# Two alternating single-column Newton chains for the norm's 1/std in a two-layer decoder trunk

## The chip, the cores and the metric

The kernel runs on one core of one Trainium2 chip. The metric is the device time of one execution in microseconds. Lower is better.

## What is computed

The reference is a trunk of two layers over 256 tokens of 2048 features, in float32. Each layer computes three branches from one input product (stick-breaking attention, a diagonal state-space model with a GLU, and cross-attention to 256 memory tokens), merges them with sigmoid gates, multiplies by `w_o`, normalises, then runs a SwiGLU feed-forward part of width 5632 and normalises again. So there are four layer norms, and the change lies in them alone:

```python
def _layer_norm(x, g, b):
    xf = x.astype(jnp.float32)
    mu = jnp.mean(xf, axis=-1, keepdims=True)
    var = jnp.mean(jnp.square(xf - mu), axis=-1, keepdims=True)
    return ((xf - mu) * lax.rsqrt(var + LN_EPS) * g + b).astype(x.dtype)
...
x = _layer_norm(DN_ALPHA * x + mix_out, ln1_g[l], ln1_b[l])
...
x = _layer_norm(DN_ALPHA * x + ffn_out, ln2_g[l], ln2_b[l])
```

## The kernel before

The 256 tokens are two blocks of 128 partitions (`TT = 2`). Weights come in as chunks of 1 MB (`raw`) and are split into a rounded part (`hi`, on ScalarE, L631) and a remainder (`lo`, on VectorE, L986), so that TensorE can multiply float32 values as pairs of faster products; the activations are split in the same way (`xs`). A layer goes through the phases U, BR, BL, GLU, G, WO and FF; FF takes 11 turns. Every engine has its own program, written out by hand, and they meet at semaphores: `.then_inc(s, 1)` raises one when an instruction has completed, `wait_ge(s, n)` holds the engine that waits. Nothing is scheduled by a tool.

The state-space part of BR and BL (`scan_states`, L1208 and on; L1230 and L1238) is of use for reading this change. It runs two independent scans `e = 0, 1` on VectorE, alternating, and each instruction waits only for the instruction of its own scan, two or more positions back. All of its instructions take a `[128, 1]` multiplier from the tile `pw` as a per-partition scalar (called a pointer scalar here); an immediate is a number that stands in the instruction.

A norm stands at the end of WO (`norm(l, 0)`) and at the end of FF (`norm(l, 1)`). On VectorE (`norm`, L1031 and on) it runs as follows. The sums of the last token blocks are added to `rows` and their statistics taken (L1145 or L1143, and L1154). Two `bn_aggr` (L1045) give mean and variance of the two token blocks, `mv[:, m, :]`. From there to the end of the Newton steps all work is on tiles of 128 x 2, one column for each token block: `var` = variance + eps (L1047), a first guess `r` by integer arithmetic on its bits (L1049), and three Newton steps of three instructions (L1051 to L1053), r <- r (1.5 - 0.5 var r r). `lnk` makes each of them raise the semaphore `ln_step` and makes the next one wait for it, so this is one chain:

```python
for _ in range(3):
    lnk(dve.scalar_tensor_tensor(out=t, in0=r, scalar=-0.5, in1=r, op0=ALU.mult, op1=ALU.mult))
    lnk(dve.tensor_tensor(u, t, var, ALU.mult))
    lnk(dve.scalar_tensor_tensor(out=r, in0=u, scalar=1.5, in1=r, op0=ALU.add, op1=ALU.mult))
```

L1071 then makes `rv[:, 4, :]` = -mean r. VectorE normalises token block 0 in six pieces (`centre`, L1079) and ScalarE block 1 (L711, which waits for `LN_STEPS * (v + 1)` counts of `ln_step`). TensorE transposes the normalised rows (`turn`, L1582), VectorE and ScalarE apply gain and bias (L1086, L718) and split (L726, L1091), and the next phase's first products (L1503 to L1505, or L1611 and L1612) follow block by block.

What TensorE does while the norm's statistics are taken differs. In `norm(l, 0)` it has 24 products with an identity whose results nobody reads (L1860). In `norm(0, 1)` it multiplies the memory tokens for the next layer (L1488, L1491). In the last norm, `norm(1, 1)`, there are no transposes: VectorE subtracts the mean and multiplies by the gain (L1058) for six of eight pieces, ScalarE makes a diagonal matrix from r (L955, after `LN_STEPS * 4 - 1` counts), TensorE first puts the bias into its banks (L1880) and then adds the product of that diagonal and the pieces (L1884), ScalarE copies out (L958), SyncE stores (L491). VectorE finishes the other two pieces alone (L1058, L1068, stored at L494).

Of the kernel before, what the change touches and what calls it, by code (L numbers as in the profile page):

```python
# [12 lines left out]
ALU = mybir.AluOpType  # L13
# [4 lines left out]
TT = T // P  # L18
# [51 lines left out]
def chunk_no(ph, l, i, c):  # L70
    return i * len(PHASES[ph][1]) + (l * CH_LAYER + CH_BASE[ph] + c)
# [29 lines left out]
HALF_CREDIT = HLS  # L101
TILE_CREDIT = 2

LN_STEPS = 14
SUMS_WO, SUMS_FF = 6, 4
SUMS_LAYER = SUMS_WO + 11 * SUMS_FF + 2
GATES = ((0, 0, 0), (1, 2, 4), (2, 3, 5))
# [6 lines left out]
def trunk(nc, x, mem, w_in, b_in, sb_w_out, lam_re_d, lam_im_d, log_dt_d, b_re_d, b_im_d, c_re_d,  # L114
# [3 lines left out]
    with ctx:  # L118
# [3 lines left out]
        def sem(name):  # L122
            return ctx.enter_context(nc.semaphore(name))
# [144 lines left out]
        stats_done, ln_step, norm_done, ln_T = sem("stats_done"), sem("ln_step"), sem("norm_done"), sem("ln_T")  # L268
# [12 lines left out]
        def norm_cols(l, which, k):  # L281

            if which == 0:
                return par[:, l, 80 + k:81 + k], par[:, l, 96 + k:97 + k]
            return par[:, 2, 32 * l + k:32 * l + k + 1], par[:, 2, 32 * l + 16 + k:32 * l + 17 + k]
# [4 lines left out]
        def next_chunk(ph, l, i, c):  # L290

            if c + 1 < len(PHASES[ph][1]):
                return ph, l, i, c + 1
            if PHASES[ph][0] > 1:
                return ph, l, i + 1, 0
            return ORDER[ORDER.index(ph) + 1], l, 0, 0
# [49 lines left out]
        def piece(t, m, c):  # L346
            return t[:, m, 512 * c:512 * c + 512]
# [275 lines left out]
        def _(act):  # L623
# [78 lines left out]
            def norm(l, which):  # L702
# [4 lines left out]
                def centre(q):  # L707
                    y = rows[:, 1, CENTRES[q]:CENTRES[q + 1]]
                    if q == 0:
                        act.wait_ge(ln_step, LN_STEPS * (v + 1))  # L710
                    act.activation(y, y, ACT.Identity, bias=rv[:, 4, 1:2], scale=rv[:, 1, 1:2]).then_inc(norm_act, 1)  # L711
# [240 lines left out]

            act.wait_ge(ln_step, LN_STEPS * 2 * DEPTH - 1)
            for m in range(TT):
# [7 lines left out]
        def _(dve):  # L962
# [21 lines left out]
            def lo_half(slot, s, h, gh):  # L984
                dve.wait_ge(hi_ready, gh + 1)
                dve.tensor_tensor(lo[:, s, :], raw[:, slot, h * HALF:(h + 1) * HALF], hi[:, s, :].bitcast(F32),  # L986
                                  ALU.subtract).then_inc(lo_ready, 1)
# [45 lines left out]
            def norm(l, which):  # L1033
                v = 2 * l + which
                base = LN_STEPS * v
                k = [0]

                def lnk(ins):
                    k[0] += 1
                    ins.then_inc(ln_step, 1)  # L1040
                    dve.wait_ge(ln_step, base + k[0])

                dve.wait_ge(stats_done, 8 * v + 8)
                for m in range(TT):
                    lnk(dve.bn_aggr(mv[:, m, :], st[:, m, :, :].rearrange("p a b -> p (a b)")))  # L1045
                var, r, t, u = rv[:, 0, :], rv[:, 1, :], rv[:, 2, :], rv[:, 3, :]
                lnk(dve.tensor_scalar(var, mv[:, :, 1], EPS, None, ALU.add))  # L1047

                lnk(dve.tensor_scalar(r.bitcast(I32), var.bitcast(I32), -0.5, float(0x5f3759df), ALU.mult, ALU.add))  # L1049
                for _ in range(3):  # L1050
                    lnk(dve.scalar_tensor_tensor(out=t, in0=r, scalar=-0.5, in1=r, op0=ALU.mult, op1=ALU.mult))  # L1051
                    lnk(dve.tensor_tensor(u, t, var, ALU.mult))
                    lnk(dve.scalar_tensor_tensor(out=r, in0=u, scalar=1.5, in1=r, op0=ALU.add, op1=ALU.mult))  # L1053
                if v == 2 * DEPTH - 1:

                    def scaled(m, c):
                        y = piece(rows, m, c)
                        dve.scalar_tensor_tensor(out=y, in0=y, scalar=mv[:, m, 0:1], in1=piece(raw, 0, c),  # L1058
                                                 op0=ALU.subtract, op1=ALU.mult).then_inc(dve_affine, 1)

                    dve.wait_ge(gb_in, 32)
                    for j, (m, c, _) in enumerate(PE_PIECES):
                        scaled(m, c)
                    for j, (m, c) in enumerate(DVE_PIECES):
                        scaled(m, c)
                        dve.wait_ge(dve_affine, len(PE_PIECES) + 2 * j + 1)
                        y = piece(rows, m, c)
                        dve.scalar_tensor_tensor(out=y, in0=y, scalar=rv[:, 1, m:m + 1], in1=piece(raw, 1, c),  # L1068
                                                 op0=ALU.mult, op1=ALU.add).then_inc(dve_affine, 1)
                    return  # L1070
                lnk(dve.scalar_tensor_tensor(out=rv[:, 4, :], in0=mv[:, :, 0], scalar=-1.0, in1=r, op0=ALU.mult,  # L1071
                                             op1=ALU.mult))
                assert k[0] == LN_STEPS
                ph, i, c = ("U", 0, 0) if which else ("FF", 0, 0)
                nxt = next_chunk(ph, l + which, i, c)

                def centre(q):
                    y = rows[:, 0, CENTRES[q]:CENTRES[q + 1]]
                    dve.tensor_scalar(y, y, mv[:, 0, 0:1], rv[:, 1, 0:1], ALU.subtract, ALU.mult).then_inc(norm_done, 1)  # L1079

                def affine(k):
                    g, b = norm_cols(l, which, k)
                    dve.wait_ge(ln_T, 16 * v + k + 1)
                    if k >= 4:
                        dve.wait_ge(xs_lo, 16 * v + k - 3)
                    dve.tensor_scalar(xf[:, k % 4, :], bank[k % 4][:, 0:T], g, b, ALU.mult, ALU.add  # L1086
                                      ).then_inc(aff_dve, 1)

                def lo_part(k):
                    dve.wait_ge(xs_hi, 16 * v + k + 1)  # L1090
                    dve.tensor_tensor(xs[:, k, T:2 * T], xf[:, k % 4, :], xs[:, k, 0:T].bitcast(F32), ALU.subtract  # L1091
                                      ).then_inc(xs_lo, 1)

                def split(h):
                    lo_half(PHASES[nxt[0]][1][nxt[3]], hl_slot(ph, c + 1, h), h,
                            chunk_no(ph, l + which, i, c) * 2 + (2 + h))

                def second_pair(h):
                    lo_half(PHASES["FF"][1][2], hl_slot("FF", 2, h), h, chunk_no("FF", l, 0, 2) * 2 + h)

                centre(0)
                centre(1)
                affine(0)
                if which:
                    split(0)
                centre(2)
                for k in range(2, KD, 2):
                    affine(k)
                    lo_part(k - 2)
                    lo_part(k - 1)  # L1110
                    if k < 6:
                        centre(2 + k // 2)
                    if k == 4 and not which:
                        split(0)
                    if k == 8:
                        split(1)
                    if k == 12 and not which:
                        second_pair(0)
                lo_part(KD - 2)
                lo_part(KD - 1)  # L1120
                if not which:
                    second_pair(1)
# [44 lines left out]
            for l in range(DEPTH):  # L1167
# [190 lines left out]
                for t in range(4):  # L1358
# [5 lines left out]
                    if l + t > 0:  # L1364
                        dve.wait_ge(glu_lo, 4 * l + t)
                    dve.scalar_tensor_tensor(out=acc[:], in0=bran[:, 1, :], scalar=1.0, in1=bran[:, 0, :],
                                             op0=ALU.add, op1=ALU.mult).then_inc(glu_m, 1)
                    dve.wait_ge(glu_hi, 4 * l + t + 1)
                    dve.scalar_tensor_tensor(out=ssmT[:, t, T:2 * T], in0=acc[:], scalar=0.5,
                                             in1=ssmT[:, t, 0:T].bitcast(F32), op0=ALU.mult,  # L1370
                                             op1=ALU.subtract).then_inc(glu_lo, 1)
# [26 lines left out]
                for i in range(2):  # L1398
# [9 lines left out]
                    else:  # L1408
                        last_sums("WO", l, 1, 7, 4, 1.0 if l else ALPHA)
                norm(l, 0)  # L1410

                last_l = l == DEPTH - 1
# [60 lines left out]
                with dve.Fori(1, 10) as i:  # L1473
                    ffn_turn(i, False, False)
                ffn_turn(10, False, True)
                norm(l, 1)


# [408 lines left out]
def hl_slot(ph, c, h):  # L1887

    return (2 * c + h) % HLS
# [26 lines left out]
```

## Time and profile before

| | us |
|---|---|
| median of 3 runs | 3010.62 (3010.21 to 3011.47) |
| the profiled execution | 3008.55 |
| its span | 3006.8 |
| TensorE busy | 2958.4 (98%) |
| VectorE busy | 2062.7 (69%) |
| ScalarE busy | 1468.9 (49%) |

The span runs from the first to the last instruction of the profiled execution; the device time of that execution has 1.75 us more around it. Granted clock is the share of the full TensorE clock that the chip allowed, 0.997 over the span. In timelines the first column is the start in us from the span's start, the second the time from the first start to the last end of a merged row, and xN says how many instructions are merged in it.

### The profile page before, as it was taken

How to read it: one execution, taken by the hardware profiler on the slowest of the kernel's cores; microseconds unless marked ns; L12 is line 12 of the kernel's file. 1: busy time of each engine (PE TensorE's matmuls, PEld its weight loads, DVE VectorE, ACT ScalarE, POOL GpSimd, SP SyncE). 2: the span in 40 equal slices, each digit the busy share in tenths (PEclk: the TensorE clock that was granted, in tenths of full speed). 3: DMA queues.
4: the chain of work that ended last, by engine and by line, in shares of the span. 5: the costliest groups of instructions: out<-in, count | busy, mean ns of one | idle time of the engine just before them, and what ended most of it. 6: DMA issues, size and time to landing. Idle time of an engine off the chain costs nothing.

```text
span 3006.8 us, 46802 instructions
## 1 busy us (share of the span) xinstructions
PE 2958.4 (98%) x16222; PEld 2536.1 (84%) x16222; DVE 2062.7 (69%) x3163; ACT 1468.9 (49%) x1975; POOL 129.8 (4%) x191
## 2 busy tenths in 40 slices
PE   6999999999999999999999999999999999999999
PEld 5888888888888888888878888888888888888887
DVE  5999766665766565655699996666767656555666
ACT  4556555454544444444455655555435444444443
POOL 5000011110000000000000000001000000000000
PEclk9999999999999999999999999999999999999999
DMA  8656567676565555555556566776765555555554
GB/s 275 170 157 172 154 181 198 178 206 211 204 204 195 195 188 188 182 195 195 168 155 160 158 169 169 195 194 179 218 218 182 189 188 182 195 195 183 191 186 153
DMA packets 672970, 562.17 MB, mean 187 GB/s; under 512 B 20761, under 2 KB 637569, under 8 KB 671873
## 3 DMA queue, kind: packets, MB, share of 16 engines
q1 hardware_dynamic: 668688, 548.48, 60.5%
q10 hardware_dynamic: 4208, 12.74, 1.1%
q8 instruction: 43, 0.70, 0.1%
q14 instruction: 31, 0.25, 0.0%
HBM read 552.78 MB, written 8.39 MB: 187 GB/s over the span
## 4 chain that ended last, share of the span: by engine, by line
PE 92%; DVE 5%; POOL 1%; ACT 1%; issue 1%; ACTq 0%; DMA 0%; DVEq 0%; POOLq 0%
PE banks L1488 22%; PE banks L1503 22%; PE banks L1491 11%; PE banks L1505 11%; PE banks L1513 7%; PE banks L1514 7%; PE banks L1515 7%; PE banks L1781 2%; DVE lo L986 1%; PE banks L1783 1%; DVE st L1154 1%; DVE scan_t L1230 0%; DVE rows L1143 0%; DVE blocks L1238 0%; POOL sc L317 0%
## 5 line engine op out<-in xcount | busy, mean ns | idle before, releaser
L986 DVE TENSOR_TENSOR lo<-raw,hi 128x1024 fp32r<-128x1024 f32 x1016 | 1222.3, 1239 | 427.5 <-ACT hi L631 397.9
L631 ACT ACTIVATE hi<-raw 128x1024 fp32r<-128x1024 f32 x884 | 904.9, 1053 | 542.1 <-PE banks L1505 288.0
L1503 PE MATMUL banks<-xs,hi 128*128 128x512 f32 x2816 | 886.4, 396 | 2.9 <-DVE xs L1091 2.9
L1488 PE MATMUL banks<-xs,hi 128*128 128x512 f32 x2544 | 807.6, 399 | 6.6 <-DVE lo L986 4.7
L1505 PEld LDWEIGHTS banks<-xs,lo 128*128 128x128 f32 x2816 | 529.0, 188 | 124.8
L1491 PEld LDWEIGHTS banks<-xs,lo 128*128 128x128 f32 x2544 | 479.0, 188 | 113.3
L1505 PE MATMUL banks<-xs,lo 128*128 128x256 f32 x2816 | 553.4, 278 | 0.0
L1491 PE MATMUL banks<-xs,lo 128*128 128x256 f32 x2544 | 501.2, 278 | 0.0
L1503 PEld LDWEIGHTS banks<-xs,hi 128*128 128x128 f32 x2816 | 430.0, 189 | 5.7 <-DVE xs L1091 3.9
L1488 PEld LDWEIGHTS banks<-xs,hi 128*128 128x128 f32 x2544 | 388.9, 189 | 14.6 <-issue 8.2
L1513 PE MATMUL banks<-hi,hT 128*128 128x512 f32 x704 | 274.0, 389 | 0.0
L1514 PE MATMUL banks<-lo,hT 128*128 128x512 f32 x704 | 274.0, 389 | 0.0
L1515 PE MATMUL banks<-hi,hT 128*128 128x512 f32 x704 | 273.9, 389 | 0.0
L656 ACT ACTIVATE tmp<-banks,par 128x256 f32<-128x256 f32 x144 | 68.2, 473 | 328.7 <-PE banks L1491 328.7
L1143 DVE TENSOR_TENSOR rows<-rows,banks 128x1024 f32<-128x1024 f32 (+1 forms) x98 | 109.5, 1152 | 117.7 <-PE banks L1515 117.7
L643 ACT ACTIVATE hi<-raw 128x1024 fp32r<-128x1024 f32 x132 | 134.8, 1052 | 79.6 <-PE banks L1515 79.6
L1515 PEld LDWEIGHTS banks<-hi,hT 128*128 128x128 f32 x704 | 132.2, 188 | 27.5
L1513 PEld LDWEIGHTS banks<-hi,hT 128*128 128x128 f32 x704 | 132.1, 188 | 26.7
L1514 PEld LDWEIGHTS banks<-lo,hT 128*128 128x128 f32 x704 | 132.2, 188 | 26.6
L999 DVE SCALAR_TENSOR_TENSOR gate<-banks,tmp 128x256 f32<-128x256 f32 x96 | 40.8, 425 | 126.6 <-ACT tmp L656 126.6
L937 ACT ACTIVATE pt<-banks 128x512 f32<-128x512 f32 x88 | 52.6, 598 | 152.3 <-PE banks L1505 152.3
L1513 PE MATMUL banks<-hi,mT 128*128 128x512 f32 x256 | 99.9, 390 | 1.5 <-DVE lo L986 1.5
(216 smaller groups left out, 2603.1 us busy)
## 6 DMA issues: line engine op xcount, KB each, us to landing
raw<-in_ffn_w_gate_up SPq DMA_DIRECT2D x176, 1024.0 KB, 5.1
raw<-in_w_in SPq DMA_DIRECT2D x160, 1024.0 KB, 7.6
raw<-in_ffn_w_down SPq DMA_DIRECT2D x88, 1024.0 KB, 5.3
raw<-in_w_o SPq DMA_DIRECT2D x32, 1024.0 KB, 5.3
raw<-in_mem_w_kv SPq DMA_DIRECT2D x16, 1024.0 KB, 5.7
raw<-in_sb_w_out SPq DMA_DIRECT2D x32, 512.0 KB, 4.1
raw<-in_ssm_w_out SPq DMA_DIRECT2D x32, 256.0 KB, 4.5
raw<-in_mem_w_out SPq DMA_DIRECT2D x32, 256.0 KB, 4.8
```

Of the source, the lines that this page charges most:

```text
L631: act.activation(hi[:, hl_slot(ph, c, h), :], raw[:, slot, h * HALF:(h + 1) * HALF], ACT.Copy).then_inc(hi_ready, 1)
L643: act.activation(hi[:, hl_slot(ph, c + 1, h), :], raw[:, slot, h * HALF:(h + 1) * HALF], ACT.Copy).then_inc(hi_ready, 1)
L656: ins = act.activation(tmp[:, k % 2, :], src[:, 0:T], ACT.Identity, bias=bias, scale=scale)
L986: dve.tensor_tensor(lo[:, s, :], raw[:, slot, h * HALF:(h + 1) * HALF], hi[:, s, :].bitcast(F32), ALU.subtract).then_inc(lo_ready, 1)
L1143: dve.tensor_tensor(y2, y2, src, ALU.add).then_inc(rows_out, 1)
L1488: pe.matmul(dst[:, :], hi[:, s, k * P:(k + 1) * P], x_t[:, k0 + k, :], start=first and k == 0, stop=False)
L1491: ins = pe.matmul(dst[:, 0:T], lo[:, s, k * P:(k + 1) * P], x_t[:, k0 + k, 0:T], start=False, stop=last and k == 7)
L1503: pe.matmul(bank[base + j], hi[:, s, at[j]], xs[:, k, :], start=k == 0, stop=False)
L1505: ins = pe.matmul(bank[base + j][:, 0:T], lo[:, s, at[j]], xs[:, k, 0:T], start=False, stop=last)
L1513: pe.matmul(dst, xh, hi[:, s, w], start=first, stop=False)
L1514: pe.matmul(dst, xh, lo[:, s, w], start=False, stop=False)
L1515: return pe.matmul(dst, xl, hi[:, s, w], start=False, stop=last)
```

## The change

The product with the variance moves out of the steps: `u` = -0.5 var is made once (L1050), and a step is then t = r u r (L1056) and r = (t + 1.5) r (L1062). Both are issued for each of the two columns by itself, and `u[:, c]` is now a pointer scalar of L1056. Each instruction waits for all but the one right in front of it, so that the columns form two chains that alternate. The first of all, and what follows behind the last, waits for everything. A norm counts 18 steps instead of 14 (12 + 1 in place of 9), which moves the thresholds that ScalarE waits for.

```diff
-LN_STEPS = 14
+LN_STEPS = 18
...
-                for _ in range(3):
-                    lnk(dve.scalar_tensor_tensor(out=t, in0=r, scalar=-0.5, in1=r, op0=ALU.mult, op1=ALU.mult))
-                    lnk(dve.tensor_tensor(u, t, var, ALU.mult))
-                    lnk(dve.scalar_tensor_tensor(out=r, in0=u, scalar=1.5, in1=r, op0=ALU.add, op1=ALU.mult))
+                lnk(dve.tensor_scalar(u, var, -0.5, None, ALU.mult))
+                for step in range(3):
+                    for m in range(TT):
+                        c = slice(m, m + 1)
+                        dve.wait_ge(ln_step, base + (k[0] if step == 0 and m == 0 else k[0] - 1))
+                        k[0] += 1
+                        dve.scalar_tensor_tensor(out=t[:, c], in0=r[:, c], scalar=u[:, c], in1=r[:, c], op0=ALU.mult,
+                                                 op1=ALU.mult).then_inc(ln_step, 1)
+                    for m in range(TT):
+                        c = slice(m, m + 1)
+                        dve.wait_ge(ln_step, base + k[0] - 1)
+                        k[0] += 1
+                        dve.scalar_tensor_tensor(out=r[:, c], in0=t[:, c], scalar=1.5, in1=r[:, c], op0=ALU.add,
+                                                 op1=ALU.mult).then_inc(ln_step, 1)
+                dve.wait_ge(ln_step, base + k[0])
```

On VectorE, the instructions of the first norm from the first guess to the first normalised piece stand in this order before (`rv` holds var, r, t and u, each of two columns; the names in brackets are the semaphores waited for):

```order
L1049 TENSOR_SCALAR rv<-rv 128x2 [waits ln_step]
L1051 SCALAR_TENSOR_TENSOR rv<-rv 128x2 [waits ln_step]
L1052 TENSOR_TENSOR rv<-rv 128x2 [waits ln_step]
L1053 SCALAR_TENSOR_TENSOR rv<-rv 128x2 [waits ln_step]
L1051 SCALAR_TENSOR_TENSOR rv<-rv 128x2 [waits ln_step]
L1052 TENSOR_TENSOR rv<-rv 128x2 [waits ln_step]
L1053 SCALAR_TENSOR_TENSOR rv<-rv 128x2 [waits ln_step]
L1051 SCALAR_TENSOR_TENSOR rv<-rv 128x2 [waits ln_step]
L1052 TENSOR_TENSOR rv<-rv 128x2 [waits ln_step]
L1053 SCALAR_TENSOR_TENSOR rv<-rv 128x2 [waits ln_step]
L1071 SCALAR_TENSOR_TENSOR rv<-mv,rv 128x2 [waits ln_step]
L1079 TENSOR_SCALAR rows<-rows,mv,rv 128x128 [waits ln_step]
```

The same place in the changed kernel, where later lines have moved down by 11 (L1071 is L1082, L1079 is L1090):

```order
L1049 TENSOR_SCALAR rv<-rv 128x2 [waits ln_step]
L1050 TENSOR_SCALAR rv<-rv 128x2 [waits ln_step]
L1056 SCALAR_TENSOR_TENSOR rv<-rv 128x1 [waits ln_step] x2
L1062 SCALAR_TENSOR_TENSOR rv<-rv 128x1 [waits ln_step] x2
L1056 SCALAR_TENSOR_TENSOR rv<-rv 128x1 [waits ln_step] x2
L1062 SCALAR_TENSOR_TENSOR rv<-rv 128x1 [waits ln_step] x2
L1056 SCALAR_TENSOR_TENSOR rv<-rv 128x1 [waits ln_step] x2
L1062 SCALAR_TENSOR_TENSOR rv<-rv 128x1 [waits ln_step] x2
L1082 SCALAR_TENSOR_TENSOR rv<-mv,rv 128x2 [waits ln_step]
L1090 TENSOR_SCALAR rows<-rows,mv,rv 128x128 [waits ln_step]
```

Nine chained instructions have become thirteen, one of two columns and twelve of one; nothing else on VectorE or on another engine has moved.

## Rows read from the trace of the kernel before

**Rows 1.** The page's busy times and its chain that ended last.
```profile
PE 2958.4 (98%) x16222; PEld 2536.1 (84%) x16222; DVE 2062.7 (69%) x3163; ACT 1468.9 (49%) x1975; POOL 129.8 (4%) x191
...
PE 92%; DVE 5%; POOL 1%; ACT 1%; issue 1%; ACTq 0%; DMA 0%; DVEq 0%; POOLq 0%
```

**Rows 2.** Timeline of the first norm: start us, us, engine, line, operation [idle before <- releaser].
```profile
772.44 5.76 PE L1860 MATMUL banks<-xs,ident_r 128*128 128x512 f32 x24
...
775.63 0.17 DVE L1049 TENSOR_SCALAR rv<-rv 128x2 int32<-128x2 int32 x1
775.83 0.16 DVE L1051 SCALAR_TENSOR_TENSOR rv<-rv 128x2 f32<-128x2 f32 x1
...
777.59 0.16 DVE L1071 SCALAR_TENSOR_TENSOR rv<-mv,rv 128x2 f32<-128x2 f32 x1
777.79 1.80 ACT L711 ACTIVATE rows<-rows,rv 128x128 f32<-128x128 f32 x3 [2.71 <-DVE rv L1071]
...
778.43 0.41 PE L1582 MATMUL banks<-ident,rows 128*128 128x128 f32 x2 [0.23 <-ACT rows L711]
```

**Rows 3.** VectorE groups by line and form: count | busy us, mean ns | idle before.
```profile
L1454 DVE SCALAR_TENSOR_TENSOR hh<-hh,uu 128x512 f32<-128x512 f32 x44 | 30.4, 692 | 4.7
...
L1058 DVE SCALAR_TENSOR_TENSOR rows<-rows,mv,raw 128x512 f32<-128x512 f32 x8 | 5.5, 747 | 0.0
...
L1053 DVE SCALAR_TENSOR_TENSOR rv<-rv 128x2 f32<-128x2 f32 x12 | 1.9, 161 | 0.4
...
L1238 DVE SCALAR_TENSOR_TENSOR blocks<-blocks,pw,scan_t 128x64 f32<-128x64 f32 x320 | 69.3, 278 | 0.0
```

**Rows 4.** VectorE's timeline in one scan, two steps of the two alternating chains.
```profile
202.97 0.62 DVE L1230 SCALAR_TENSOR_TENSOR scan_t<-blocks,pw 128x128 f32<-128x128 f32 x2
203.50 0.88 DVE L1238 SCALAR_TENSOR_TENSOR blocks<-blocks,pw,scan_t 128x64 f32<-128x64 f32 x4
204.28 0.62 DVE L1230 SCALAR_TENSOR_TENSOR scan_t<-blocks,pw 128x128 f32<-128x128 f32 x2
```

**Rows 5.** VectorE's timeline elsewhere: neighbours not chained, without a pointer scalar.
```profile
200.37 0.42 DVE L999 SCALAR_TENSOR_TENSOR qm_f<-banks,tmp 128x256 f32<-128x256 f32 x1
200.70 2.36 DVE L986 TENSOR_TENSOR lo<-raw,hi 128x1024 fp32r<-128x1024 f32 x2
```

**Rows 6.** Timeline of the third norm, TensorE's cover and what follows it.
```profile
2249.43 5.76 PE L1860 MATMUL banks<-xs,ident_r 128*128 128x512 f32 x24
...
2255.41 0.41 PE L1582 MATMUL banks<-ident,rows 128*128 128x128 f32 x2 [0.23 <-ACT rows L711]
```

**Rows 7.** Timeline of the second norm, TensorE's cover and what follows it.
```profile
1519.81 0.39 PE L1491 MATMUL banks<-mT,lo 128*128 128x256 f32 x2
...
1520.84 0.41 PE L1582 MATMUL banks<-ident,rows 128*128 128x128 f32 x2 [0.63 <-ACT rows L711]
```

**Rows 8.** Timeline of the last norm and the end of the kernel.
```profile
2991.44 5.31 PE L1880 MATMUL banks<-raw,ident 128*128 128x512 f32 x12
...
2995.86 4.73 DVE L1058 SCALAR_TENSOR_TENSOR rows<-rows,mv,raw 128x512 f32<-128x512 f32 x7
...
2996.16 0.59 PE L1880 MATMUL banks<-raw,ident 128*128 128x512 f32 x1
2996.76 0.67 PE L1884 MATMUL banks<-rows,diag 128*128 128x512 f32 x1
...
3002.80 0.33 SPq L491 DMA_DIRECT2D out_x<-rows  x1
3003.18 0.96 SPq L494 DMA_DIRECT2D out_x<-rows  x2
```

**Rows 9.** Windows, first and second norm: busy PE, PEld, DVE, ACT, POOL, granted clock, DMA.
```profile
780.00:784.00 4.00, 3.28 (x21) 2.97 (x22) 3.60 (x9) 3.97 (x10) 0.00 (x0) 1.00 0.91 393
...
1520.00:1524.00 4.00, 1.90 (x12) 1.04 (x11) 3.61 (x8) 3.52 (x8) 0.00 (x0) 0.97 0.00 0
1524.00:1528.00 4.00, 3.74 (x17) 3.41 (x18) 3.77 (x10) 3.59 (x8) 0.00 (x0) 0.60 0.00 0
```

## The prediction

> **What bounds the kernel now.** I read the page's busy times and its chain first, then the timelines of the four norms, then the VectorE groups by form, and last a stretch where this kernel already runs two alternating chains. TensorE is busy 98% of the span and holds 92% of the chain that ended last; VectorE holds 5% [rows 1]. The norms belong to those 5%: TensorE cannot go on before they have given it rows. In the first norm the Newton steps run from 775.83 to 777.59 us with no other work on VectorE, ScalarE waits 2.71 us for the instruction behind them, and TensorE starts its transposes at 778.43, released by ScalarE's first piece [rows 2]. So this code is on the path in every norm, and what is won or lost there is won or lost in the time, as long as TensorE's own cover does not end later.
>
> How much there is to win is plain from the same rows: nine instructions in 777.59 - 775.83 = 1.76 us, or 0.196 us each [rows 2]. One takes 0.161 us [rows 3]; 0.035 us more pass until the next one, which waited for it, starts. Four norms hold 4 x 1.76 = 7.0 us, 0.23% of the time. Even if all of it went, the kernel would gain hardly more than the 0.2% (6.0 us) from which a measurement of this kernel can tell a difference from no change.
>
> **The change, part by part.** Removed: nine chained instructions a norm, 1.76 us.
>
> Added, L1050: one two-column instruction with an immediate, chained to both neighbours. Its twin L1049 starts 775.83 - 775.63 = 0.20 us ahead of its successor [rows 2]. **+0.20 us.**
>
> Added, twelve single columns in two chains. This needs two prices for each kind: the latency (how soon an instruction that waits for it can start), and the spacing (how soon any next one can).
>
> *Latency.* L1062 has only immediates and one column. The two-column L1053 takes 0.161 us, and a column costs about (692 - 161) / 510 = 1.04 ns [rows 3], so one column fewer is worth 1 ns: 0.160 + 0.035 = 0.195, say 0.196 us. L1056 has a pointer scalar. With 512 columns that form takes 747 ns against 692 with an immediate, and with 64 columns 278 against 161 + 62 x 1.04 = 226 [rows 3]: 52 to 55 ns more. The trace has no pointer form of one column; I carry 52 ns down to it, 0.160 + 0.052 = 0.212 us, and 0.248 with the wait. Bounds: 0.196 (no surcharge at this width) and 0.248.
>
> *Spacing.* Here the scan is the same code pattern. Two L1230 of 128 columns and four L1238 of 64 make a step, and it takes 204.28 - 202.97 = 1.31 us [rows 4]. The first L1238 starts 0.53 us behind the first of two L1230, so 0.265 us each; the four L1238 take 0.78, or 0.195 each, though one lasts 0.278 [rows 3, 4]. So neighbours overlap by 0.083 us, also those that carry a wait for the other's predecessor. At 1.04 ns a column both spacings are 0.13 us plus the columns; the 512-column L1058 gives (4.73 - 0.75) / 6 = 0.663, also 0.13 plus the columns [rows 8]. Without a pointer scalar the constant is smaller: L986 starts 0.33 us behind L999, which has 256 columns [rows 5]: 0.06 to 0.07. For one column: **0.131 us behind L1056, 0.065 behind L1062.** Whether so small an instruction can follow as closely is unknown; the lower bound is 0.065 for both, the upper one no overlap at all, which is the slow rival below.
>
> *The schedule of a step* (starts in us, t and r for L1056 and L1062, columns 0 and 1). t0 at 0, t1 at 0.131. r0 must be 0.131 behind t1 and 0.248 behind t0: 0.262. r1 must be 0.065 behind r0 and 0.248 behind t1: 0.379. The next t0 waits for r0: 0.262 + 0.196 = 0.458. A step takes 0.458 us against 3 x 0.196 = 0.588 before. The last r1 starts at 2 x 0.458 + 0.379 = 1.295, and L1082 waits for it: 1.295 + 0.196 = 1.49. With L1050 the block takes **1.69 us against 1.76: 0.07 us less a norm.** The saved third instruction is paid back by the pointer scalar, by the offset of the second chain and by L1050.
>
> *What that does behind the block.* In the first norm TensorE's filler products, 24 in all, end at 772.44 + 5.76 = 778.20, and the transposes start at 778.43; the third norm has the same distance, 2255.41 - 2255.19 = 0.22 [rows 2, 6]. So 0.07 passes in full, and nothing above 0.23 would. In the second norm the cover ends at 1520.20 and the transposes start at 1520.84 [rows 7]: room for 0.64. In the last one L1884 starts at 2996.76, 0.15 behind the end of the first L1058 (2995.86 + 0.75), and the last of twelve L1880 starts at 2996.16, (2996.16 - 2991.44) / 11 = 0.43 apart, so it is out of the way by 2996.59: room for 0.17 [rows 8]. The stores follow in SyncE's order, the last two at 3003.18, behind one of 0.33 us issued at 3002.80 that waits for ScalarE, hence for TensorE [rows 8]; VectorE's and TensorE's paths move together. The prefetches, loads and semaphores are unchanged: no queue is passed. ScalarE's new thresholds name the same instructions.
>
> **Sum:** 4 x (1.76 - 1.69) = 0.28 us less. Against the profiled execution that is 3008.55 - 0.28 = 3008.27; that execution was 2.07 us below the median of the runs, so for the median 3010.62 - 0.28 = **3010.3 us**.
>
> **A rule that speaks against it.** The scan's step of 1.31 us holds six pointer instructions whose durations add up to 2 x 0.355 (0.62 less the spacing) + 4 x 0.278 = 1.82 us [rows 3, 4], so they overlap at 64 and 128 columns. The Trainium skill (VectorE: DVE Perf Modes, section on the DRAIN, and its rules for authors) says that a chain of VectorE instructions pays a pipeline flush each whether or not they wait for each other, and to keep the count of operations low rather than that of semaphores; a neighbouring section of the same page lets a following instruction that is not held start earlier. By the first rule thirteen in place of nine can only lose; by these rows it fails at 64 columns, and none shows it at one.
>
> **The rivals.**
> *No overlap at one column (slower).* Every one of the twelve waits out its predecessor as if chained: 6 x 0.248 + 6 x 0.196 + 0.20 = 2.86 us, 1.10 more than before; four norms give +4.4 us, 3015.0. For it: every short instruction in this trace that stands close to others is chained, so none shows an overlap; the skill's rule would give this. Against: [rows 4]. Two periods stand in the block, so it breaks even when a step takes 0.458 + 0.07 / 2 = 0.49 us; four durations end to end (2 x 0.212 + 2 x 0.160 = 0.74) would be far beyond that. A loss has no cover in any norm and passes in full.
> *Cheap columns (faster than I say).* No pointer surcharge and 0.065 spacing: period 0.392, last r1 at 0.784 + 0.261, the block 1.44 us, 0.32 less. TensorE's covers cut this to 0.23 + 0.32 + 0.23 + 0.17 = 0.95 us: 3009.7. Against: the surcharge is the same at 64 and 512 columns, so it is not one per column.
> *The clock.* In the second norm the granted clock falls to 0.60 in 1524 to 1528 [rows 9], behind a stretch of 4 us in which TensorE was busy 1.90. That is a stretch mostly at 1.2 instead of 2.4 GHz; 4 us at a mean of 0.60 do the work of 2.4, so a dip costs at most 1.6 us. A start that moves by 0.07 us could end this dip or bring one in another norm: 3008.7 or 3011.9. Against: in the first norm the same place ran at 1.00 [rows 9], and 0.07 us is little beside the idle time there, 4.00 - 3.28.
> *Nothing moves at all* is not apart from the forecast in the time; the trace would tell them apart.
>
> **How the numbers follow.** Overlap as in the scan, 0.28 us less: 0.72. Cheap columns: 0.08. No overlap, +4.4: 0.10. The clock, 1.6 either way: 0.08. Something unseen: 0.02. The range starts from the runs themselves, since 0.28 us is smaller than their own spread: the lowest time seen for this kernel is 3008.55 and the highest 3011.47. Low: 3008.55 - 0.28, rounded to 3008.3. High: 3011.47 + 1.6 = 3013.1. It leaves out the case without overlap, and no more than a tenth beside it. All cases lie within 6.0 us of before, so the chances are 0.01 faster, 0.97 same, 0.02 slower, the last for a cost that no row shows.
>
> **What would show it.** In the changed profile: L1056 at about 212 ns and L1062 at 160, the start of the first L1056 to the start of L1082 1.49 us, a step 0.46; L1082 to the first transpose unchanged at 0.84 us; in each norm the transposes 0.07 earlier behind the last statistics. Starts of neighbours 0.25 and 0.20 apart throughout would show the first rival; 0.07 apart the second. Wrong altogether would be a block longer than 1.76 us, or a time outside the range with a block near 1.69, which would put the cause elsewhere.

## The result and the profile after

| | before | changed |
|---|---|---|
| median of 6 runs, us | 3011.05 (3009.03 to 3012.36) | 3022.64 (3020.33 to 3025.82) |
| ratio, 95% interval | | 1.0039 (1.0029 to 1.0049) |
| span of the profiled execution, us | 3006.8 | 3024.1 |

By the medians the change makes the kernel 11.6 us slower (0.39%). The forecast was 3010.3 us, 0.28 us faster, with a range of 3008.3 to 3013.1. The two profiled executions lie 17.3 us apart, because that of before was among the fastest of its kernel and that of the changed kernel the slowest of its own (3025.82).

The place that was forecast first. VectorE's timeline of the first norm in the changed kernel, which answers to [rows 2]:

```profile
778.88 0.17 DVE L1049 TENSOR_SCALAR rv<-rv 128x2 int32<-128x2 int32 x1
779.09 0.17 DVE L1050 TENSOR_SCALAR rv<-rv 128x2 f32<-128x2 f32 x1
779.37 0.35 DVE L1056 SCALAR_TENSOR_TENSOR rv<-rv 128x1 f32<-128x1 f32 x2
779.63 0.28 DVE L1062 SCALAR_TENSOR_TENSOR rv<-rv 128x1 f32<-128x1 f32 x2
779.84 0.34 DVE L1056 SCALAR_TENSOR_TENSOR rv<-rv 128x1 f32<-128x1 f32 x2
...
780.55 0.28 DVE L1062 SCALAR_TENSOR_TENSOR rv<-rv 128x1 f32<-128x1 f32 x2
780.86 0.16 DVE L1082 SCALAR_TENSOR_TENSOR rv<-mv,rv 128x2 f32<-128x2 f32 x1
```

From the first L1056 to L1082 it is 780.86 - 779.37 = 1.49 us, as forecast, and two chains do run side by side: two L1056 of 0.215 us each (the groups below) end within 0.35. But 0.28 us pass from L1050 to L1056, not 0.20. The block takes 1.77 us where before took 1.76: the change gains nothing at its own place and loses nothing there. The 11.6 us are elsewhere.

The trace's records have one instruction more here than the order listing ahead of the prediction, which isn't counted as busy and so stands in no timeline: a wait by itself (L1054) between L1050 and the first L1056. `lnk` puts a wait behind L1050, and the first turn of the step loop puts the same wait ahead of L1056; an instruction carries one of the two, the other becomes an instruction of its own. So a norm has not four instructions more but five.

I looked for the 11.6 us with the waits. VectorE's waits in which the profile shows nothing that it waited for, first before, then changed (line waited: us in total, times, longest):

```profile
DVE sp_t L1246 <- issue: 5.3, 8, 0.8
DVE scan_t L1230 <- issue: 1.4, 2, 0.7
DVE pw L1257 <- issue: 0.8, 4, 0.2
```
```profile
DVE pw L1268 <- issue: 14.5, 4, 7.3
DVE sp_t L1257 <- issue: 5.0, 7, 0.8
DVE scan_t L1241 <- issue: 1.4, 2, 0.7
```

L1257, now L1268, is the first copy in the body of the branch loop (`dve.Fori(0, 3)`, phase BR). The change doesn't touch it. Its two long waits are at the two branches back of layer 1. VectorE's timeline before:

```profile
1603.98 0.42 DVE L999 SCALAR_TENSOR_TENSOR u_f<-banks,tmp 128x256 f32<-128x256 f32 x1
1604.39 0.42 DVE L1251 TENSOR_TENSOR sbT<-banks,sbT 128x256 f32 x1
...
1605.02 0.21 DVE L1257 COPY pw<-powers 128x96 f32 x1 [0.20 <-issue]
...
1669.72 0.42 DVE L999 SCALAR_TENSOR_TENSOR u_f<-banks,tmp 128x256 f32<-128x256 f32 x1
...
1735.47 0.42 DVE L999 SCALAR_TENSOR_TENSOR u_f<-banks,tmp 128x256 f32<-128x256 f32 x1
```

and in the changed kernel:

```profile
1607.24 0.42 DVE L999 SCALAR_TENSOR_TENSOR u_f<-banks,tmp 128x256 f32<-128x256 f32 x1
1607.65 0.42 DVE L1262 TENSOR_TENSOR sbT<-banks,sbT 128x256 f32 x1
1615.41 0.21 DVE L1268 COPY pw<-powers 128x96 f32 x1 [7.33 <-issue]
...
1679.50 0.42 DVE L999 SCALAR_TENSOR_TENSOR u_f<-banks,tmp 128x256 f32<-128x256 f32 x1
1679.91 0.42 DVE L1262 TENSOR_TENSOR sbT<-banks,sbT 128x256 f32 x1
1687.07 0.21 DVE L1268 COPY pw<-powers 128x96 f32 x1 [6.73 <-issue]
...
1751.16 0.42 DVE L999 SCALAR_TENSOR_TENSOR u_f<-banks,tmp 128x256 f32<-128x256 f32 x1
```

L999 on `u_f` stands near the end of each turn, so its distances are turns: before 65.74 and 65.75 us, changed 72.26 and 71.66. That is 6.5 + 5.9 = 12.4 us more, which is the loss by the medians (11.6) and somewhat over. Of the 17.3 us between the profiled executions, 3.3 lie ahead of this loop and 1.6 behind it. Of the 3.3, 1.7 stand already at the end of the last turn of this loop in layer 0, up to where VectorE's programs are alike; the other 1.6 and the 1.6 behind go with two dips of the granted clock, from 346.0 and from 1837.7 us, that `b_shift10` (below) has as well. TensorE feels it as a wait for the split weights and then runs slowly for a while (timeline of TensorE, changed kernel, then two windows with the granted clock behind POOL's column):

```profile
1612.38 0.63 PE L1499 MATMUL banks<-xs,hi 128*128 128x512 f32 x2
1612.85 0.39 PE L1502 MATMUL banks<-xs,lo 128*128 128x256 f32 x2
1616.84 1.22 PE L1499 MATMUL banks<-mT,hi 128*128 128x512 f32 x2 [3.60 <-DVE lo L986]
...
1618.29 1.05 PE L1499 MATMUL banks<-mT,hi 128*128 128x512 f32 x2
```
```profile
1612.00:1616.00 4.00, 1.24 (x8) 0.91 (x6) 0.59 (x2) 2.55 (x4) 0.00 (x0) 0.98 0.05 13
1616.00:1620.00 4.00, 3.16 (x10) 2.68 (x11) 4.00 (x9) 1.19 (x3) 0.00 (x0) 0.50 0.14 34
```

What a branch back could wait for is its own code. The page lists a DMA queue of the kind "instruction" (packets, MB); over 1560 to 1800 us, before and changed:

```profile
q14 instruction: 5, 0.04, 0.1%
```
```profile
q14 instruction: 15, 0.12, 0.2%
```

Ten more fetches of 8 KB. By the trace's packet records they are exactly those of the two turns: between one branch back and the next the changed kernel has five packets of this queue in either turn, before has none. Two of the five fall into the stall itself. With 64 bytes to an instruction (so the Trainium skill, Perfetto Trace Analysis, section on the 4-stage abstract model; no run here shows it by itself) one fetch is 128 instructions; that size is tested below by positions alone.

So the theory before the experiments: the change makes VectorE's program longer, five instructions a norm, ten ahead of the branch loop of layer 1. That loop is 302 instructions long. By the records of VectorE's trace, with each loop ahead counted once, 1032 instructions stood ahead of it, and 1042 do now. Code comes in blocks of 128; a loop whose body touches three of them stays in reach, one that touches four is fetched again at each branch back. A body of 302 touches four when its first instruction is at 83 to 127 of its block (counted from 0), 45 of 128 positions (the expectation of shift 60 says 46, and the sentence is off by that one). The rivals: the new chains or their semaphores cost the time; the norm's shifted end moves later loads; or any growth of the code costs.

### The profile page after: what moved, and what is told of

It is laid out like the page before. It is cut to its first block, busy times and chain, and to the rows that moved or that the text cites. A ratio compares the mean times of both kernels' runs of the same rounds, so it can differ in the third digit from the quotient of the medians.

```text
span 3024.1 us, 46822 instructions
## 1 busy us (share of the span) xinstructions
PE 2967.9 (98%) x16222; PEld 2543.1 (84%) x16222; DVE 2056.5 (68%) x3179; ACT 1469.8 (49%) x1975; POOL 144.2 (5%) x191
## 4 chain that ended last, share of the span: by engine, by line
PE 88%; DVE 7%; issue 2%; ACT 1%; POOL 1%; DMA 0%; ACTq 0%; DVEq 0%; POOLq 0%
PE banks L1514 22%; PE banks L1499 20%; PE banks L1516 11%; PE banks L1502 10%; PE banks L1524 7%; PE banks L1526 7%; PE banks L1525 7%; DVE lo L986 2%; PE banks L1792 2%; PE banks L1794 1%; DVE blocks L1249 1%; DVE scan_t L1241 1%; DVE st L1165 1%; DVE scan L1249 1%; DMA tab_save<-stage 0%
## 5 line engine op out<-in xcount | busy, mean ns | idle before, releaser
L986 DVE TENSOR_TENSOR lo<-raw,hi 128x1024 fp32r<-128x1024 f32 x1016 | 1215.3, 1232 | 426.3 <-ACT hi L631 396.5
L999 DVE SCALAR_TENSOR_TENSOR gate<-banks,tmp 128x256 f32<-128x256 f32 x96 | 40.8, 424 | 134.2 <-ACT tmp L656 134.2
```

## The experiments

**The code's position without the change.** `b_shift10` is the kernel before with idle instructions on VectorE. Two waits make one instruction (the trace has ten records more), so 20 waits make the ten; the other shifts of this kind differ in that number alone.

```diff
+                if l == 0:
+                    for _ in range(20):
+                        dve.wait_ge(masks, 8)
                 ffn_turn(0, True, False)
                 with dve.Fori(1, 10) as i:
```

> The kernel before, with ten idle instructions on VectorE (waits that are long fulfilled) ahead of the feed-forward loop of layer 0, so that every later VectorE instruction stands at the position that the change gives it at the branch loop of layer 1. Newton steps untouched. Theory 1 (the code's position decides: at its back branch that loop must be fetched again): VectorE idles 6 to 7.5 us at the loop's head at two of its branches back, and the time rises by 10 to 13 us over before. Rival (the new chains or their semaphores cost the time, or the norm's new timing shifts the loads): no such idle time, the time of before within 1 us.

Measured: 3023.9 us against 3011.36, ratio 1.0041 (1.0027 to 1.0055). The timeline at the first branch back of layer 1:

```profile
1608.58 0.42 DVE L1251 TENSOR_TENSOR sbT<-banks,sbT 128x256 f32 x1
1615.66 0.21 DVE L1257 COPY pw<-powers 128x96 f32 x1 [6.65 <-issue]
```

The old Newton steps with ten instructions that do nothing reproduce the whole loss. The chains are not its cause.

**The chains without the position.** `a_layer1_only` uses them in the two norms of layer 1, behind that loop:

```diff
-LN_STEPS = 14
+LN_BASE = (0, 14, 28, 46, 64)
...
+                if l == 0:
+                    for _ in range(3):
+                        lnk(dve.scalar_tensor_tensor(out=t, in0=r, scalar=-0.5, in1=r, op0=ALU.mult, op1=ALU.mult))
...
+                else:
+                    lnk(dve.tensor_scalar(u, var, -0.5, None, ALU.mult))
```

> The new chains in the two norms of layer 1 alone, which stand behind the branch loop of layer 1; layer 0 keeps the old steps. Theory 1: no idle time at that loop, time as before within 1 us. Rival (the chains themselves cost): half of the loss, 5 to 6 us.

Measured: 3012.44 us against 3011.36, ratio 1.0003 (0.9993 to 1.0012). At the loop's head:

```profile
1605.26 0.21 DVE L1274 COPY pw<-powers 128x96 f32 x1 [0.20 <-issue]
```

No half of the loss; the median is 1.1 us up, inside the interval.

**The change further down.** `a_shift60` is the changed kernel with 50 idle instructions (100 waits) at the place above, so that the loop stands 60 behind its place in before.

> The changed kernel with 50 idle instructions more on VectorE at that place, so that the branch loop of layer 1 stands 60 instructions later than before. Theory 1 with fetch blocks of 128 or 256 instructions, of which the loop of 302 may touch only so many: a shift of 47 to 56 beyond the critical point is out of the bad band (its width would be 128 x 3 - 302 subtracted from 128, 46 instructions), so no idle time at the back branch, and the time of before within 1.5 us. Rival (the chains cost, or any growth of the code costs): the time of the change, 11 to 12 us over before, or more.

Measured: 3011.73 us against 3011.36, ratio 1.0003 (0.9993 to 1.0013).

```profile
1608.95 0.21 DVE L1268 COPY pw<-powers 128x96 f32 x1 [0.24 <-issue]
```

The longest code of the three timed kernels has no long wait. It is not growth that costs but where the loop comes to lie.

**One block further.** `b_shift138`: the kernel before, with 276 waits at the same place.

> The kernel before with 138 idle instructions at that place, 128 more than in the first kernel of this set. Theory 1 with blocks of 128 instructions: the idle time of 6 to 7 us at two back branches returns. With blocks of 256 instructions: none. The instructions themselves cost at most 4 us of VectorE time ahead of a stretch where it has slack, 0 to 2 us of the kernel's time.

Measured: one run, 3034.7 us, and at the first branch back

```profile
1623.85 0.21 DVE L1257 COPY pw<-powers 128x96 f32 x1 [6.97 <-issue]
```

The second has 6.95 us from the branch to the next instruction. The long waits are back at a distance of 128 from the shift of ten: the blocks are 128, not 256. The idle instructions themselves were dearer than I expected, 12.6 us in one wait of L986 <- issue, 0.09 us each, for which TensorE has one wait of 8.1 us. That accounts for most of the 10.8 us above the 3023.9 of shift 10; with one run the rest is open. In shift 60 the same wait was 4.0 us for 50.

**The edges.** `b_shift5` (10 waits, what one norm adds) and `b_shift50` (100 waits).

> The kernel before with five idle instructions at the same place: what the change adds in one norm. With blocks of 128 instructions and a bad band of 46 positions, whose edge lies 1 to 10 instructions behind the loop's position in before, either this kernel has the two idle times of 6 to 7 us at the back branch or the next one (shift 50) has them, and never both or neither, since the band's lower edge is reached at 5 exactly when its upper edge is not left before 51. A rival rule (any position later than some point is bad) would have them in both.

> The kernel before with fifty idle instructions at the same place: see shift 5. About 4 us of VectorE time for the idle instructions themselves, as in the kernel with shift 60, of which little shows in the time.

Measured: 3010.01 us and 3019.37 us, one run each. The heads of the loop, shift 5 and then shift 50:

```profile
1606.52 0.21 DVE L1257 COPY pw<-powers 128x96 f32 x1 [0.19 <-issue]
```
```profile
1612.86 0.21 DVE L1257 COPY pw<-powers 128x96 f32 x1 [5.81 <-issue]
```

One of the two, as the blocks of 128 demand. With shift 10 bad and shift 5 good, the loop of before starts at 73 to 77 of its block. One norm alone could have taken the change; the second brought it over the edge. Without the doubled wait of each norm the shift would have been 8, at 81 to 85 of the block with the edge at 83: whether it stalls there is open.

**Both layers.** `b_start40` has the idle instructions at VectorE's very start, ahead of the branch loop of layer 0 too:

```diff
-            dve.wait_ge(masks, 8)
+            for _ in range(80):
+                dve.wait_ge(masks, 8)
             dve.tensor_copy(ident_r[:], ident[:]).then_inc(consts, 1)
```

> The kernel before with 40 idle instructions on VectorE at its very start, so that the branch loops of both layers move by 40. From the blocks of 128: the loop of layer 0 stands 22 positions ahead of that of layer 1 within a block, so both lie in the bad band now: four idle times of 6 to 7 us, two in each layer, and 22 to 28 us over before, plus up to 4 us for the idle instructions at the start. Rival (something in layer 1 alone, such as its loads or its counts on the semaphores): the idle times stay in layer 1 or do not come.

Measured: one run, 3028.69 us, 18 over before. The four heads:

```profile
134.72 0.21 DVE L1258 COPY pw<-powers 128x96 f32 x1 [6.46 <-issue]
...
205.37 0.21 DVE L1258 COPY pw<-powers 128x96 f32 x1 [6.87 <-issue]
...
1623.32 0.21 DVE L1258 COPY pw<-powers 128x96 f32 x1 [5.83 <-issue]
...
1693.11 0.21 DVE L1258 COPY pw<-powers 128x96 f32 x1 [5.94 <-issue]
```

Layer 0, which never waited here before, now does: nothing in layer 1's data or counts is needed. (The expectation has this loop 22 positions ahead of the other within a block. By the trace's records it is 1032 - 117 = 915 instructions, so 19; with either number it comes to lie in the bad band.) The time is 4 us under my estimate: the four waits add up to 25.1 us of VectorE's time, and what kept a part of that off the path was not taken apart.

All positions together, in an ordinary table (shift of the loop against before; instructions ahead of the loop; time from the start of the branch to the start of the next instruction, and packets of 8 KB until the next branch, both at the two branches back, from the trace's records):

```
layer, shift       instructions ahead   gaps, us       packets   kernel
1,   0              1032                 0.29  0.28     0  0      before
1,   0              1032                 0.29  0.28     0  0      a_layer1_only
1, -10              1022                 0.30  0.28     0  0      a_u_first (below)
1, -10              1022                 0.30  0.28     0  0      a_u_beside (below)
1,   5              1037                 0.28  0.27     0  0      b_shift5
1,  10              1042                 7.06  6.46     5  5      changed
1,  10              1042                 6.38  6.51     5  5      b_shift10
1,  40              1072                 5.92  6.04     5  5      b_start40
1,  50              1082                 5.90  5.33     5  5      b_shift50
1,  60              1092                 0.33  0.29     0  0      a_shift60
1, 138              1170                 6.69  6.95     5  5      b_shift138
0,   0               117                 0.34  0.31     0  0      before
0,  40               157                 6.55  6.97     5  5      b_start40
```

Every stalled turn has five fetches and no other turn has one, so a wait for code is what the stall is. Blocks of 64 would fit the shifts of layer 1 too, but not layer 0: its loop of before, 915 instructions ahead, would stand by blocks of 64 where a shift of 45 stands, in the middle of shifts that stall, and it doesn't.

**A version without the stall, and the 0.08 us.** `a_u_first` keeps the chains and takes instructions off VectorE ahead of both loops, and it makes u ahead of the first guess, so that the first L1056 no longer takes its scalar from the instruction in front of it:

```diff
         def _(pool):
             pool.memset(ident[:], 0.0).then_inc(masks, 1)
+            for s, v in ((y_done, 4), (bu_copied, 2), (ks_step, 1), (gelu_step, 5), (sp_step, 2), (tri_done, 1),
...
+                pool.sem_inc(s, v)
...
-                dve.sem_inc(s, v)
...
+                lnk(dve.tensor_scalar(u, var, -0.5, None, ALU.mult))
                 lnk(dve.tensor_scalar(r.bitcast(I32), var.bitcast(I32), -0.5, float(0x5f3759df), ALU.mult, ALU.add))
-                lnk(dve.tensor_scalar(u, var, -0.5, None, ALU.mult))
```

> The changed kernel with two edits. The 20 additions to semaphores at VectorE's start are issued by GpSimd, which takes 20 instructions off VectorE ahead of both branch loops: no idle time at a back branch in either layer by the blocks of 128. And u = -0.5 var is made before the first guess r instead of behind it, so that the first instruction of the chains no longer takes its pointer scalar from the instruction in front of it: if that was the cost of 0.08 us there (0.28 us from L1050 to L1056 in the changed kernel against 0.20), the block is 1.69 us in place of 1.77; if it is the cost of any pointer form behind a wait, 1.77 stays. Time: that of before less 0.3 us by the one, equal by the other; 11 us more if the chains and not the position were the cause.

Measured: 3010.72 us against 3010.55, ratio 1.0001 (0.9992 to 1.001). The first norm:

```profile
778.06 0.17 DVE L1050 TENSOR_SCALAR rv<-rv 128x2 int32<-128x2 int32 x1
778.35 0.35 DVE L1056 SCALAR_TENSOR_TENSOR rv<-rv 128x1 f32<-128x1 f32 x2
```

No stall, and the loss is gone with the chains in place. The 0.08 us stay, 0.29 from the guess to L1056, though its scalar is one instruction older. So it is not the scalar's age. Nor is it the pointer form behind a wait, the other case of the expectation: in before, L1079 takes two pointer scalars, the second from the Newton steps, waits for L1071 right in front of it, and starts 777.79 - 777.59 = 0.20 us behind it like any other. L1068, which has the form of L1056 and waits for the L1058 in front of it, starts 0.035 us behind its end.

```profile
777.59 0.16 DVE L1071 SCALAR_TENSOR_TENSOR rv<-mv,rv 128x2 f32<-128x2 f32 x1
777.79 0.74 DVE L1079 TENSOR_SCALAR rows<-rows,mv,rv 128x128 f32<-128x128 f32 x2
```

What stands between in the changed kernel, here and in the next version is the wait by itself. It starts 0.21 us behind the instruction in front, about where a chained instruction would start, and L1056 starts 0.076 us behind it, in all three. That it costs the 0.08 us is read from these records; no run left it out. Inside the chains there is no such instruction and no 0.08 (L1062 to the next L1056: 779.84 - 779.63 = 0.21).

**One link less.** `a_u_beside` takes u from the variance directly, beside `var`:

```diff
-                lnk(dve.tensor_scalar(var, mv[:, :, 1], EPS, None, ALU.add))
-
+                k[0] += 1
+                dve.tensor_scalar(var, mv[:, :, 1], EPS, None, ALU.add).then_inc(ln_step, 1)
+                k[0] += 1
+                dve.tensor_scalar(u, mv[:, :, 1], EPS, -0.5, ALU.add, ALU.mult).then_inc(ln_step, 1)
+                dve.wait_ge(ln_step, base + k[0] - 1)
                 lnk(dve.tensor_scalar(r.bitcast(I32), var.bitcast(I32), -0.5, float(0x5f3759df), ALU.mult, ALU.add))
-                lnk(dve.tensor_scalar(u, var, -0.5, None, ALU.mult))
```

> As the kernel before this one (chains, semaphore additions on GpSimd), but u = -0.5 (variance + eps) is taken from bn_aggr's result beside var and not behind it: one link less in the chain. From the start of L1047 to the start of the instruction behind the last Newton step, before takes 2.17 us and the changed kernel 2.18; here 0.20 less 0.065 of spacing goes, so 2.04 to 2.05 in each of four norms. That is 0.5 us of the time, 3010.1 where before has 3010.6, less than a measurement of this kernel can tell: the block in the profile is what decides. No idle time at a back branch. If a pointer form behind a full wait costs 0.08 us more than an immediate one whatever its scalar's age, 0.28 us stay between the first guess and the first L1056-form.

Measured: 3009.99 us against 3010.74, ratio 0.9999 (0.999 to 1.0008).

```profile
775.61 0.17 DVE L1048 TENSOR_SCALAR rv<-mv 128x2 f32<-128x2 f32 x1
775.69 0.16 DVE L1050 TENSOR_SCALAR rv<-mv 128x2 f32<-128x2 f32 x1
775.82 0.17 DVE L1052 TENSOR_SCALAR rv<-rv 128x2 int32<-128x2 int32 x1
776.10 0.35 DVE L1058 SCALAR_TENSOR_TENSOR rv<-rv 128x1 f32<-128x1 f32 x2
...
777.59 0.16 DVE L1084 SCALAR_TENSOR_TENSOR rv<-mv,rv 128x2 f32<-128x2 f32 x1
```

From `var` to the end 1.98 us, where the changed kernel has 2.18 and before 2.17. I had expected 2.04 to 2.05: u lies wholly in the 0.2 us that the guess waits for `var` anyway, so its spacing costs nothing. The 0.28 us from the guess to the first of the chains are here too, with the wait by itself in them. This is the best version seen: in the profile 4 x 0.19 = 0.76 us better than before at its own place; the medians differ by as much (0.75), but their interval holds no difference at all, so that it is faster is not shown.

## Why the prediction was wrong

**The step that failed** is a sentence of the part on what lies behind the block: "The prefetches, loads and semaphores are unchanged: no queue is passed." I counted data and forgot that instructions are loaded too. My range of causes was closed over what happens in the norms and what they pass on, so the 11.6 us had no case; "something unseen" had a chance of 0.02, and "slower by over 0.2%" too. What the runs showed in its place: VectorE's program grows by ten instructions ahead of a loop of 302, and at both branches back of that loop VectorE waits for code, 7.06 and 6.46 us instead of 0.3. The order listing that stands ahead of the prediction showed the cause openly, but for the doubled waits: nine instructions become thirteen, and every later one moves. The trace before held the rest: a loop of 302 instructions on VectorE, an instruction queue with 8 KB packets.

The Trainium skill (Runtime: NRT & Kernel Launch, section on instruction fetch mechanics) has the rule that the prediction lacked: an engine holds a small window of its code, and a taken branch whose target lies outside it must fetch first. In kind the traces here agree, by the gaps of 5.3 to 7.1 us at two branches back against 0.3. The same section of the Trainium skill has the window made of two blocks of 256 instructions. By that a body of 302 would reach into a third block at 45 starts in a row out of 256, so that shifts 10 and 138 could not both stall, and they do. The measurement decides: 128.

**Newton block, 1.69 us forecast, 1.77 measured.** The term that failed is one that the sum has not got. L1050, "+0.20 us", measures 0.21 to what follows it, but what follows is the doubled wait as an instruction of its own, which the prediction put at nothing, and L1056 starts 0.076 us behind that: 0.28 together. Less this 0.08 the block is at the 1.69 of the forecast. The prices of the rest held. L1056 takes 0.215 us (0.212 forecast), L1062 0.156 (0.160), groups by form of the changed kernel:

```profile
L1056 DVE SCALAR_TENSOR_TENSOR rv<-rv 128x1 f32<-128x1 f32 x24 | 4.2, 215 | 0.5
L1062 DVE SCALAR_TENSOR_TENSOR rv<-rv 128x1 f32<-128x1 f32 x24 | 3.3, 156 | 0.0
```

The step is 0.47 and 0.45 us (0.458), the chains 1.49 (1.49). Two L1056 start 0.13 us apart (0.131), so carrying the scan's spacing [rows 4] down to one column was right there. The 0.065 behind an L1062 was not put to the test: in the schedule another wait always ends later, and the neighbours are 0.08 to 0.12 apart.

**The rival of no overlap** falls by the same rows: it had neighbours 0.20 to 0.25 us apart. Its direction was "slower" and so was the result, but by another mechanism at another place. The prediction's "thirteen in place of nine can only lose" fails at one column as well: the twelve of the chains take 1.49 us where nine chained ones took 1.76. **The rival of cheap columns** falls too: the surcharge of a pointer scalar is there at one column. **The clock** is not a cause of its own here. In the profile of the changed kernel the granted clock is 0.50 in four stretches where that of before has 1.00: 3.4 us from 346.0, 6.8 from 1615.8, 6.8 from 1687.5 and 3.4 from 1837.7. `b_shift10`, with the old Newton steps, has four at the same places, so the chains bring none of them, and the first lies ahead of every norm. The second and third follow the two stalls, in which TensorE had little to do (1.24 of 4 us in the window above), and lie inside the 12.4 us.

**What passes on to TensorE:** L1082 to the first transpose, which TensorE starts at 781.70, is 781.70 - 780.86 = 0.84 us, as forecast.

## What to carry to other kernels

An edit that adds or takes away instructions ahead of a loop moves the loop in its engine's code. Waits count too: two waits in a row in front of one instruction are an instruction more. Before costing the edit, note the length of every later loop on that engine and where it lies, and ask whether a shift could bring it over a block more; the waits named "issue" at a loop's first instruction tell at once. And when an edit of some nanoseconds moves a kernel by microseconds, run the old code with idle instructions in place of the new ones before believing anything about the edit.

## What the runs showed that I had not expected

A loop of 300 or 302 instructions on VectorE costs 0.3 us at its branch back or 5.3 to 7.1, depending on its start within 128 instructions. The data fit a reach of three blocks; why three, and whether the code fetched ahead is what pushes the first block out, was not tried. The length of a stall is settled in part. In all twelve the next instruction starts 1.6 us behind the end of the last packet that lands in the stall (1.59 to 1.65, from the trace's packet records), and that packet, or the one directly in front of it, starts 3.3 to 5.0 us behind the branch. What holds it for so long is open: in the changed kernel the DMA engines carried some 290 GB/s of other data until 1612.5 us, while the loop's head waited, but before had as much traffic there, and no run took it away. At shift 50, where only one to five of the loop's instructions lie in its first block, the gaps were the shortest.

A pointer scalar costs an instruction 0.05 to 0.06 us of duration at 1, 64 and 512 columns (215 ns against 156 at one, 278 against the 226 worked out at 64, 747 against 692 at 512). A wait isn't free when it is an instruction of its own: one that carries two long fulfilled waits takes 0.09 us of VectorE's program (12.6 us for 138), and the doubled wait of a norm 0.076.
